# Value products per head with both halves of the values as one stationary operand, in a two-layer attention and ConvFFN kernel

## What is computed

```
a = jnp.where(visible, jnp.exp(jax.nn.log_sigmoid(z) + suffix), 0.0)      # stick-breaking, strictly causal
o_sb = jnp.einsum('bhqk,bkhd->bqhd', a.astype(v.dtype), v)
p = jax.nn.softmax(jnp.where(visible, s, -jnp.inf), axis=-1)              # latent attention, causal by chunks of 64
o_lat = jnp.einsum('bhqk,bkl->bqhl', p.astype(c_kv.dtype), c_kv)
o_mla = jnp.einsum('bthl,lhv->bthv', o_lat, w_uv)
```

## Time and profile before

| | us |
|---|---|
| median of 3 runs (1854.4 to 1856.71) | 1856.55 |
| the profiled execution | 1855.66 |
| its span | 1853.8 |
| PE busy | 1830.7 (99%) |
| DVE, ACT, POOL busy | 927.1, 559.6, 1070.4 |

### The profile page before, as it was taken

The page is one execution under the profiler, slowest core; times in us unless marked ns, Lnnn a source line. Parts: engine busy times, 40 slices in busy tenths (PEclk is TensorE's granted clock), DMA queues, the critical chain, the costliest instruction groups (busy, mean ns, idle before and its releaser), DMA issues.

```text
span 1853.8 us, 33791 instructions
## 1 busy us (share of the span) xinstructions
PE 1830.7 (99%) x14262; PEld 1775.2 (96%) x14262; DVE 927.1 (50%) x1634; ACT 559.6 (30%) x1197; POOL 1070.4 (58%) x994
## 2 busy tenths in 40 slices
PE   9999999999999999999999999999999999999999
PEld 8998989999999999999999999899999999999999
DVE  5666775232755532523556767752336555235143
ACT  4444543112422221202344344531133222122021
POOL 7685634656555555556666854346456555555564
PEclk9999999999999999999999999999999999999999
DMA  5242212333222222223342421212422222222222
GB/s 181 95 127 73 70 41 71 101 107 125 69 92 91 82 91 92 85 80 99 97 146 89 126 75 58 69 58 92 151 81 69 92 92 82 90 92 87 80 87 94
DMA packets 76231, 170.49 MB, mean 92 GB/s; under 512 B 6384, under 2 KB 34160, under 8 KB 76080
## 3 DMA queue, kind: packets, MB, share of 16 engines
q1 hardware_dynamic: 68752, 160.79, 26.7%
q10 hardware_dynamic: 7328, 7.54, 1.2%
HBM read 156.41 MB, written 9.79 MB: 90 GB/s over the span
## 4 chain that ended last, share of the span: by engine, by line
PE 89%; DVE 5%; POOL 2%; ACT 2%; DMA 1%; issue 1%; SPq 0%; DVEq 0%; ACTq 0%; POOLq 0%
PE ps L1550 75%; PE ps L1585 2%; PE ps L1713 2%; POOL wsp L611 2%; PE ps L1671 2%; DVE xn L1083 1%; DVE xT L1422 1%; DVE mix L1419 1%; PE ps L1762 1%; PE ps L1768 1%; PE ps L1624 1%; DVE R L1083 1%; POOL wsp L605 1%; DVE xT L1240 1%; PE ps L1736 1%
## 5 line engine op out<-in xcount | busy, mean ns | idle before, releaser
L1550 PE MATMUL ps<-xn,wsp 128*128 128x272 f32 x7824 | 1003.7, 289 | 7.4 <-POOL wsp L611 2.6
L1550 PEld LDWEIGHTS ps<-xn,wsp 128*128 128x128 f32 x7824 | 986.9, 189 | 11.6 <-issue 5.5
L611 POOL TENSOR_TENSOR wsp<-raw,wsp 128x256 fp32r<-128x256 f32 (+1 forms) x578 | 726.3, 1278 | 22.3
L605 POOL CAST wsp<-raw 128x512 fp32r<-128x512 f32 (+2 forms) x372 | 319.5, 873 | 660.0 <-DMA raw<-in_wstream 565.4
L1550 PE MATMUL ps<-R,wsp 128*128 128x272 f32 x3840 | 486.2, 288 | 0.1
L1550 PEld LDWEIGHTS ps<-R,wsp 128*128 128x128 f32 x3840 | 482.7, 188 | 1.2 <-DVE xT L1112 0.5
L1083 DVE SCALAR_TENSOR_TENSOR R<-ps,R 64x256 fp32r<-64x256 f32 (+11 forms) x264 | 129.8, 510 | 77.6 <-ACT R L679 26.0
L1438 DVE TENSOR_TENSOR mix<-ps,rstd 128x272 f32<-128x272 f32 x88 | 38.8, 441 | 202.6 <-PE ps L1550 192.3
L968 ACT ACTIVATE mix<-vv 128x2 f32<-128x2 f32 x88 | 18.0, 204 | 363.0 <-DVE mix L1440 363.0
L1083 DVE SCALAR_TENSOR_TENSOR R<-mix,R 128x544 fp32r<-128x544 f32 (+2 forms) x86 | 74.7, 869 | 82.0 <-ACT R L989 66.9
L1446 DVE SCALAR_TENSOR_TENSOR ps<-mix,vv,ps 128x546 f32<-128x546 f32 x88 | 69.4, 788 | 55.6 <-ACT ps L977 55.6
(11 more groups left out here) (230 smaller groups left out, 1473.9 us busy)
## 6 DMA issues: line engine op xcount, KB each, us to landing
raw<-in_wstream SPq DMA_DIRECT2D x233, 512.0 KB, 3.5
raw<-in_wstream SPq DMA_DIRECT2D x48, 128.0 KB, 2.6
raw<-in_wstream SPq DMA_DIRECT2D x16, 384.0 KB, 3.0
raw<-in_kc SPq DMA_DIRECT2D x8, 512.0 KB, 3.7
raw<-in_vc SPq DMA_DIRECT2D x8, 512.0 KB, 4.5
xT<-in_x_in SPq DMA_DIRECT2D x8, 272.0 KB, 6.6
out_k_out<-mix ACTq DMA_DIRECT2D x8, 272.0 KB, 3.2
xT<-in_x_in SPq DMA_DIRECT2D x1, 2176.0 KB, 9.4
```

Source lines behind the costliest of these rows:

```text
L605: ins = nc.gpsimd.tensor_copy(dst[:, 0, f], part[:, f])
L611: ins = nc.gpsimd.tensor_tensor(dst[:, 1, f], part[:, f], dst[:, 0, f].bitcast(F32), ALU.subtract)
L1550: mm = pe.matmul(z[:, h], w[:, x, (k0 + k) * P:(k0 + k + 1) * P], rhs[:, y, k, h * HT:(h + 1) * HT], start=(k == 0 and (x, y) == (0, 0)), ...
```

## The change

For each head of a pair there is now one tile, `pv0` and `pv1`, over all four query blocks. The stationary operand is a key block of one head's values, its high part in 64 columns and its low part in the other 64; the moving operand is that head's weights, high part and then low part, so that two passes give all four part products. The high-value rows come out in partitions 0 to 63 and the low-value rows in 64 to 127, and DVE adds the two halves in a new operation (line 1201 of the changed kernel), behind a wait on its own low-part operation (semaphore `pv_low`). For key block kb only query blocks kb to 3 are multiplied: 512, 384, 256 and 128 columns. Both tiles stand five steps behind the pair's first unit; nothing stands three steps behind. So that each key block's weights are contiguous, the transposed weights are kept in a triangle that is interleaved for the two heads, the second one's with the query blocks in reverse; the value tiles are laid out by key block, head and part. Nothing is changed in the projections or in `FILL`. The core of the diff:

```diff
-        AHEAD = {start(br, t) + d: [("pv" + h + br, t)] for br in "sm" for t in range(PAIRS) for h, d in (("a", 3), ("b", 5))}
+        AHEAD = {start(br, t) + 5: [("pv0" + br, t), ("pv1" + br, t)] for br in "sm" for t in range(PAIRS)}
...
+        def at_keys(x, r, kb):
+
+            o = (2 * ATW // P - 4 - 3 * kb if r else 4 * kb) * P
+            return at[:, x, o:o + (QB - kb) * P]
...
                     def pv_tile(t):
...
-                        for r in range(2):
-                            ins = ac(o[64 * r:64 * r + 64, 0, t[1], q], bank(t)[64 * r:64 * r + 64, 256 * r:256 * r + 256], ACT.Copy)
-                        ins.then_inc(S["act_read"], 1)
+                        z = turned(bank(t)[0:64], r)
+                        o = (o_sb if t[0][3] == "s" else o_ml)[64 * r:64 * r + 64, 0, t[1], 0:SEQ]
+                        ac(turned(o, 0), z, ACT.Copy).then_inc(S["act_read"], 1)
...
-                        elif t > 0 and qb in (0, 2):
-                            act.wait_ge(S["p_done"], AT[(("pva" if qb == 0 else "pvb") + br, t - 1)] + 1)
+                        elif t > 0 and qb == 0:
+                            act.wait_ge(S["p_done"], AT[("pv1" + br, t - 1)] + 1)
...
-                        for r in range(2):
-                            lo(o[64 * r:64 * r + 64, 1, t[1], q], bank(t)[64 * r:64 * r + 64, 256 * r:256 * r + 256],
-                               o[64 * r:64 * r + 64, 0, t[1], q], "dve_read" if r else None)
+                        r, z = int(t[0][2]), bank(t)
+                        o = (o_sb if t[0][3] == "s" else o_ml)[64 * r:64 * r + 64, :, t[1], 0:SEQ]
+                        lo(turned(o[:, 1], 0), turned(z[0:64], r), turned(o[:, 0], 0), "pv_low")
+                        dve.wait_ge(S["pv_low"], PV_AT[t] + 1)
+                        v.tensor_tensor(turned(o[:, 1], 0), turned(z[64:128], r), turned(o[:, 1], 0).bitcast(F32),
+                                        ALU.add).then_inc(S["dve_read"], 1)
...
-                        pe.wait_ge(S["at_lo"], n + 1)
-                        z, blocks = bank(t).rearrange("p (r q) -> p r q", r=2), 2 if t[0][2] == "a" else QB
...
+                            pe.wait_ge(S["at_lo"], start(br, p) + QB)
+                        for kb in range(QB):
+                            w = (QB - kb) * P
+                            z = bank(t)[:, 0:w] if r else bank(t)[:, 512 - w:512]
+                            for x in range(2):
+                                mm = pe.matmul(z, val[:, 2 * kb + r].rearrange("p x f -> p (x f)"), at_keys(x, r, kb),
+                                               start=(kb == 0 and x == 0), stop=(kb == QB - 1 and x == 1))
```

More of the change, by code:

```diff
@@ L254, in at_view, with turned, v_parts @@
         def at_view(x, qb):
-            o = qb * (qb + 1) // 2 * P
-            return at[:, x, :, o:o + P * (qb + 1)]
+            a = at[:, x, qb * P:(qb + 1) * P]
+            return bass.AP(tensor=a.tensor, offset=a.offset,
+                           ap=[a.ap[0], [(2 * ATW // P - 1 - 5 * qb) * P, 2], [3 * P, qb + 1], [1, P]])
+        def at_keys(x, r, kb):
+            o = (2 * ATW // P - 4 - 3 * kb if r else 4 * kb) * P
+            return at[:, x, o:o + (QB - kb) * P]
+        def turned(ap, r):
+            z = ap.rearrange("p (b q) -> p b q", q=P)
+            return z[:, ::-1] if r else z
+        def v_parts(buf, i, y):
+            return buf[:, i, :, y]
         def backward(ap, n):
@@ L310, in ahead @@
             return AHEAD.get(s, [])
+        PV_AT = {t: n for n, t in enumerate([t for s in range(STEPS) for t in ahead(s) if t[0][0:2] == "pv"])}
         def after(s):
@@ L725, in vt_tile @@
                         z, new, f = bank(t), bank(t, 1)[0:DEC, 0:P], slice(t[1] * P, (t[1] + 1) * P)
-                        ac(v_s[:, t[1] % 2, 0], z.rearrange("p (b l) -> p b l", l=P), ACT.Copy)
+                        ac(v_parts(v_s, t[1] % 2, 0), z.rearrange("p (b f) -> p b f", f=64), ACT.Copy)
                         ac(v_tail[0:DEC, 0, t[1]], new, ACT.Copy)
@@ L735, in pv_tile @@
                     def pv_tile(t):
+                        if t[0] == "pv0s" and t[1] == 2:
+                            act.wait_ge(pre["qr_in"], QR_MOVES * (layer + 1))
+                        r = int(t[0][2])
                         act.wait_ge(S["p_done"], AT[t] + 1)
-                        if t[0] == "pvas" and t[1] == 2:
-                            act.wait_ge(pre["qr_in"], QR_MOVES * (layer + 1))
-                        o, q = (o_sb if t[0][3] == "s" else o_ml), slice(0, SEQ // 2) if t[0][2] == "a" else slice(SEQ // 2, SEQ)
-                        for r in range(2):
-                            ins = ac(o[64 * r:64 * r + 64, 0, t[1], q], bank(t)[64 * r:64 * r + 64, 256 * r:256 * r + 256], ACT.Copy)
-                        ins.then_inc(S["act_read"], 1)
+                        z = turned(bank(t)[0:64], r)
+                        o = (o_sb if t[0][3] == "s" else o_ml)[64 * r:64 * r + 64, 0, t[1], 0:SEQ]
+                        ac(turned(o, 0), z, ACT.Copy).then_inc(S["act_read"], 1)
                     def qn_tile(t):
@@ L757, in kv_tile @@
                         ac(kn[:, t[1] % 2, 0], bank(t), ACT.Copy)
-                        ac(vm[:, t[1] % 2, 0], bank(t, 1).rearrange("p (b l) -> p b l", l=P),
+                        ac(v_parts(vm, t[1] % 2, 0), bank(t, 1).rearrange("p (b f) -> p b f", f=64),
                            ACT.Copy).then_inc(S["act_read"], 1)
@@ L1170, in vt_tile @@
                         dve.wait_ge(S["act_read"], aread(t))
-                        lo(v_s[:, t[1] % 2, 1], bank(t).rearrange("p (b l) -> p b l", l=P), v_s[:, t[1] % 2, 0], None)
+                        lo(v_parts(v_s, t[1] % 2, 1), bank(t).rearrange("p (b f) -> p b f", f=64), v_parts(v_s, t[1] % 2, 0), None)
                         lo(v_tail[0:DEC, 1, t[1]], bank(t, 1)[0:DEC, 0:P], v_tail[0:DEC, 0, t[1]], "dve_read")
@@ L1187, in kv_tile @@
                         lo(kn[:, t[1] % 2, 1], bank(t), kn[:, t[1] % 2, 0], None)
-                        lo(vm[:, t[1] % 2, 1], bank(t, 1).rearrange("p (b l) -> p b l", l=P), vm[:, t[1] % 2, 0], "dve_read")
+                        lo(v_parts(vm, t[1] % 2, 1), bank(t, 1).rearrange("p (b f) -> p b f", f=64), v_parts(vm, t[1] % 2, 0), "dve_read")
                     def ql_tile(t):
@@ L1696, in pv @@
                     def pv(t):
-                        br, p = t[0][3], t[1]
-                        n = start(br, p) + (1 if t[0][2] == "a" else 3)
-                        val, o = (v_s if br == "s" else vm)[:, p % 2], 0 if t[0][2] == "a" else 3 * P
+                        br, p, r = t[0][3], t[1], int(t[0][2])
+                        val = (v_s if br == "s" else vm)[:, p % 2]
                         banks_free(t)
-                        if t[0][2] == "a":
+                        if r == 0:
                             pe.wait_ge(S["dve_read"], dread(("vt" if br == "s" else "kv", p)))
-                        pe.wait_ge(S["at_lo"], n + 1)
-                        z, blocks = bank(t).rearrange("p (r q) -> p r q", r=2), 2 if t[0][2] == "a" else QB
-                        for kb in range(blocks):
-                            for i, (x, y) in enumerate(PARTS):
-                                if kb == blocks - 1:
-                                    mm = pe.matmul(z[:, :, P:2 * P], val[:, x, kb], at[:, y, :, o + 2 * kb * P:o + (2 * kb + 1) * P],
-                                                   start=False, stop=(i == 2))
-                                else:
-                                    a = at[:, y, :, o:o + 2 * (blocks - 1) * P].rearrange("p r (b q) -> p r b q", b=2)
-                                    mm = pe.matmul(z.rearrange("p r (b q) -> p r b q", b=2), val[:, x, kb],
-                                                   a[:, :, :, kb * P:(kb + 1) * P], start=(kb == 0 and i == 0), stop=False)
+                            pe.wait_ge(S["at_lo"], start(br, p) + QB)
[5 more added lines that the diff above has]
+                                               start=(kb == 0 and x == 0), stop=(kb == QB - 1 and x == 1))
                         mm.then_inc(S["p_done"], 1)
```

28 lines of the change are left out of this document (15 added, 13 removed).

## The result

The changed kernel takes 1860.99 us (median of 8 runs, 1858.79 to 1862.2), the kernel before, measured beside it, 1856.72 (8 runs, 1853.09 to 1857.55). The ratio is 1.0022 with a 95% interval of 1.0013 to 1.0032: slower by 0.2%, some 4 us. The forecast was 1861.5. The profiled execution took 1862.2 us, its span is 1860.4, against 1855.66 and 1853.8 before.

The account below looks back on a forecast made before the run. PE, busy 99% of the span, was taken to bound the kernel. Matmul savings of 16.7 us, waits of 19.8 and clock loss of 3.0 gave +6.1 on 1855.66, 1861.8; the stated forecast was 1861.5, range 1851 to 1868.

Parts of the forecast that it names:

- PE's own work: Value products on PE: a pair falls from 3.64 to 2.6 us, 16.7 us less in all.
- rival 4: Value products on PE: a matmul's price hangs on its count, not its columns; 6.5 us saved, 1872; chance 0.03.
- ACT and DVE: Readers of the value products: ACT's copy 0.60 us, DVE's difference and add 0.68 each, 2.8 per pair with the link.
- Step 9: `v` 3 takes `pv1`'s bank while DVE is late: new PE waits of 5.5 and 5.9 us.
- Rival 2: DVE reaches step 9's pair early, by t + 4.6 (t: products' start): 1854.4, or 1849 with small waits halved; chance 0.16.
- Step 10: PE's waits for POOL there, 0.79 and 1.19 us, vanish, since POOL works on.
- Steps 14, 18, 27, 31, 35: PE waits added: 0.9 and 1.5 at 14 and 18, 0.6 more at 27 and 31, 0.5 more at 35 (1.3).
- Steps 4 and 13: PE waits 0.27 us there for the products of the unit before; the wait grows by 0.3 each.
- Step 5: Fill for 3 us behind the products covers DVE's chain; without that fill it would cost some 2 us.
- The 0.2 of step 31: In step 31, some 0.2 us of PE's gain is lost to waiting.
- The clock: Slower PE clock after pauses: 1.5 us per layer at step 9, 1.5 for short waits, less 1.5 before: 3.0.
- Sum: Whole kernel: -16.7 of PE work, +19.8 of waits (9.9 per layer), +3.0 of clock: +6.1 us.

Follow-up runs that it names:

- The experiment with the rotary operations: Changed kernel with DVE's four rotary operations moved from the end of step 8 to behind step 9's value products: 1848.92 us, ratio 0.9966.
- the one with the banks: Changed kernel with step 9's two free banks handed out the other way, so that `v` 3 takes over `pv0`'s: 1857.54 us, ratio 1.0007.
- the run with PE held back: Changed kernel with five unused 512-column matmuls added in steps 3 and 12 of each layer: 1861.48 us, ratio 1.0022.
- the one with the order changed: Changed kernel with ACT and DVE handling the previous unit's weights between `pv0` and `pv1` in steps 23, 27 and 31: 1861.11 us, ratio 1.0012.
- the repeated run: Changed kernel run again as it is, in the third group of runs: 1860.2 us, ratio 1.0024.
- the tuned kernel before: Kernel before with rotary operations moved behind step 9's products and, in steps 23, 27 and 31, its tile evacuated behind the scaling: 1852.58 us, ratio 0.9977.

## Why the prediction was right, step by step

- **PE's own work**: 2.6 us per pair forecast, 2.58 in steps 5 and 9. That the price follows the columns, and not the count (rival 4), is settled. The estimate from the spacings that the Trainium skill states ("TensorE: Matmul & The Clock Gate", Back-to-back issue gap) is not borne out: by it all pairs together would have saved 7 us.
- **ACT and DVE**: 0.60 and 0.68 forecast for the copy, the difference and the add; 0.592, 0.680 and 0.694 measured.
- **Step 9**: waits of 5.5 and 5.9 forecast, 5.59 and 5.41 measured, released by `pv1`'s add. The experiment with the rotary operations shows the cause, the one with the banks shows whose add it is. Rival 2 (DVE comes early) did not happen: it came at t + 6.4 and t + 6.2, with the rotary operations at 1.10 to 1.14. Other executions show a weak form of it: with the first of them at 0.73 DVE came at t + 5.5 and the wait was 4.67 or 4.68 (step 9 in one layer each of the run with PE held back and of the one with the order changed). It never came as early as the t + 4.6 from which the rival would decide.
- **Step 10**: the waits for POOL vanished, as forecast.
- **Steps 14, 18, 27, 31, 35**: 0.9, 1.5, 1.15, 1.15 and 1.3 forecast; 0.72, 1.36, 1.06, 1.07 and 1.37 measured. The 0.15 that the sum put behind the scores of steps 28 and 32 as well did not show.
- **Steps 4 and 13 were mis-sized**: "the wait grows by 0.3 each"; it grew by 0.56 (0.47 + 0.36 against 0.27). The step counted 1.14 us less on PE. But the first start behind the products also comes sooner: the six transposes and their idle 0.16 took 70.94 - 69.96 = 0.98 before and 68.83 - 68.25 = 0.58 now, and so PE arrives about 1.5 us earlier where 1.14 was counted. What PE gained beyond the sum it lost for the most part in that wait, so the total hardly changed.
- **Step 5 was called covered and is not**: 0.41 and 0.45. A wait at a covered step was among the prediction's own signs of being wrong; it is worth 0.9 us. The sum counted on 3 us of fill. DVE was late by what the three rotary operations in layer 0 took: 0.92, 1.14 and 1.02 against 0.81, 0.72 and 0.73 before, with POOL at work beside them and, before, idle for most of that time. That last link is read from the traces and was not tested. The 0.2 of step 31 did not show.
- **The clock**: 3.0 us forecast, 4.6 - 1.5 = 3.1 measured, but put together otherwise. The forecast was 1.5 per pause of step 9 and 1.5 for the short waits; the pauses cost 2.68 and 1.91, and the short waits, up to 1.37, nothing. The total was right by luck, its parts were not: the same two pauses cost 4.3 us in the repeated run, and in the runs with the other bank and with the other order no more than 1.4 to 1.5 each.
- **Sum**: per layer the new waits are 4.80 (step 9 less step 10), 0.72, 1.36, 1.03, 0.56, 1.12 and 0.41, 10.0 in layer 0 and, with 4.22 for step 9, 9.4 in layer 1, so 19.4 against 19.8. The total holds better than its parts: steps 4, 5 and 13 add 0.9 per layer to the sum, and steps 14, 18 and 27 to 31 take 1.0 off it. (The 18.5 from the view's totals are less by the four waits of 0.16 in steps 3 and 12, which are gone, and by small ones at the start of the run.) The sum has no term for the overlap that is lost at each new wait, 1.2 us of PE's busy time by what the result shows.
- **How near it came**: the two profiled executions lie 6.5 us apart, for which the sum gave 6.1. The medians lie 4.3 apart, and the forecast of 1861.5, which had set aside 1.1 of the sum by choice, is 4.8 above the kernel before. That it is within 0.5 us of the measured 1860.99 is luck in part; that the gain on PE goes whole into waits, step 9 first, is not.

## What to carry to other kernels

A saving on the engine that bounds the kernel is real only as far as the engines behind it can follow at that place. Here DVE was idle half the time, and still a new 0.69 us operation per tile cost 12 to 15 us, because it stood in a chain at whose end PE takes a bank over, or ahead of low parts that PE's next scores need. So for each tile that changes, write down three times against the start of its matmuls: when PE arrives at the next use of the bank, when the reader's queue comes to the tile, and how long the readers' chain is. When the reader's queue is late for another reason, as with the rotary operations here, move that reason before judging the change; and give the reordered version to the old kernel as well, or its share is counted as the change's.

## What the runs showed of the hardware

- **The loss of clock does not grow with the pause.** Twelve pauses of 3.2 to 5.6 us in step 9 were traced. The 48 matmuls behind them took 7.79 and 8.93 us behind two pauses of 5.59, 7.61 behind 3.75, 8.76 behind 3.71, 7.77 behind 4.68. Against 6.25 the loss lies between 1.4 and 2.7 us, with a spread from one execution to the next that is as large as between lengths. With 22 matmuls in the pause there was none.
- **A wait of 1.37 us can be free and one of 1.19 cost 1.5.** Waits of 1.35 to 1.37 in steps 9, 18 and 35 left the 48 matmuls of steps 9 and 35 at 6.24 to 6.26; waits of 1.19 and, in the tuned kernel before, 1.27 in step 10 of layer 1 were followed by 7.78. What differs in the rows is what PE does ahead of the wait: value products and nine transposes in the one case, products of 256 columns and two transposes in the other. Which of this matters was not tried.
- **DVE beside POOL.** The rotary operations, from and to SBUF, take 0.72 or 0.73 us at their shortest and mostly 1.0 to 1.15 beside POOL's splitting of weights. DVE's operations from PSUM stay at 0.65 to 0.70 beside the same work of POOL, as the second add of step 9 does (0.69 at 123.06, with POOL's line 632 from 122.04 to 124.82). DVE is not always the one that is slowed. In step 9 of layer 1 with the banks given the other way, the first rotary operation took 0.73 although POOL's pair of casts ran beside it, and it was these that took longer, 2.19 us in place of 1.16. They had begun 0.06 us after the rotary operation:

```profile
1036.08 0.73 DVE L1176 TENSOR_TENSOR mix<-mix 128x544 f32<-128x544 f32 x1
...
1036.14 2.19 POOL L627 CAST wsp<-raw 128x512 fp32r<-128x512 f32 x2
```

The Trainium skill ("SBUF — State Buffer", Who interferes with whom) has DVE and GpSimd share one pair of ports as an exclusive lock, and only DVE instructions with two SBUF inputs, or in a two-port mode, take part in it; the engine that issues second is the one that is blocked. By that rule, the trace agrees in which operations are slowed and, in these rows, in which engine gives way: in the changed kernel POOL's casts began at 1038.58, before the rotary operation at 1039.22, and it was the latter that took 1.10.
